# Eight tiles of first dots moved from ahead of the first spread into it, a quarter tile before each group

## The reference

```python
s = einsum('thpd,hpnd->thpn', (xb @ w_query), sub_keys)      # scores of 128 keys per half
top_s, top_i = top_k(s, 16)                                   # 16 best keys of each half
best_s, pos = top_k(top_s[0][:, None] + top_s[1][None, :], 16)
eid = key1 * 128 + key2                                       # expert number: two keys
gate = softmax(best_s)
z = einsum('thkd,td->thk', expert_down[eid], xb)              # the dots
out = einsum('thk,thkd->td', gate * gelu(z), expert_up[eid])  # the sums
```

## Time and profile before

| | |
|---|---|
| median of 3 runs | 4025.26 us (4020.61 to 4026.69) |
| the profiled execution, its own time | 4031.59 us |
| its span, from the first to the last instruction | 4029.8 us |
| PE busy | 3728.5 us, 93% of the span |
| DVE busy | 2323.1 us, 58% |
| ACT busy | 1266.1 us, 31% |
| share of PE in the chain that ended last | 86% |
| mean granted clock of TensorE | 0.932 of full speed |

### The profile page before, as it was taken

The page is one execution under the profiler, slowest core; times in us unless marked ns, Lnnn a source line. Parts: engine busy times, 40 slices in busy tenths (PEclk is TensorE's granted clock), DMA queues, the critical chain, the costliest instruction groups (busy, mean ns, idle before and its releaser), DMA issues.

```text
span 4029.8 us, 48913 instructions
## 1 busy us (share of the span) xinstructions
PE 3728.5 (93%) x14086; PEld 2386.4 (59%) x14086; DVE 2323.1 (58%) x4748; ACT 1266.1 (31%) x3367; POOL 658.0 (16%) x602
## 2 busy tenths in 40 slices
PE   7977999789999999997998899799589999999997
PEld 3443583576677777663444444347476677777764
DVE  1072696579877655664123400258978977755556
ACT  1141010357655454001011100101156755545201
POOL 0000001123433222220000000000113333311221
PEclk9988999669999999998997999899758999999998
DMA  3101148559999877993211112213657999977897
GB/s 131 64 20 52 63 169 362 198 204 388 379 392 400 342 298 299 396 383 133 73 63 47 42 73 73 84 61 120 258 188 289 386 377 394 391 300 301 343 384 284
DMA packets 129888, 926.81 MB, mean 230 GB/s; under 512 B 14800, under 2 KB 15744, under 8 KB 18184
## 3 DMA queue, kind: packets, MB, share of 16 engines
q0 software_dynamic: 73728, 536.90, 32.8%
q1 hardware_dynamic: 52368, 377.51, 24.4%
q10 hardware_dynamic: 3704, 11.36, 0.8%
HBM read 923.59 MB, written 2.12 MB: 230 GB/s over the span
## 4 chain that ended last, share of the span: by engine, by line
PE 86%; ACT 5%; DVE 5%; issue 2%; DMA 2%; ACTq 0%; DVEq 0%; POOL 0%; POOLq 0%; SPq 0%
PE proj L646 21%; PE proj L429 16%; PE obk L637 16%; PE tps L594 11%; PE proj L421 10%; PE proj L608 5%; ACT hot L920 2%; PE proj L578 2%; ACT hot L923 1%; DMA wring<-in_slabs 1%; PE tps L394 1%; PE obk L745 1%; DMA ring<-in_experts,idx 1%; DVE stat L1186 0%; PE proj L735 0%
## 5 line engine op out<-in xcount | busy, mean ns | idle before, releaser
L646 PE MATMUL proj<-wring,hT 128*128 128x512 f32 x2048 | 943.3, 604 | 1.8 <-DVE hT L1391 1.8
L374 POOL DMA_INDIRECT ring<-in_experts,idx x512 | 635.5, 1241 | 1766.1 <-DVE xn L1365 1655.9
L637 PE MATMUL obk<-hT,wring 128*128 128x256 f32 x3072 | 694.2, 379 | 0.0
L637 PEld LDWEIGHTS obk<-hT,wring 128*128 128x128 f32 x3072 | 583.5, 190 | 159.5 <-issue 89.5
L594 PEld LDWEIGHTS tps<-hT,hot 128*128 128x128 f32 x4096 | 601.0, 226 | 123.6 <-ACT hot L923 61.0
L594 PE MATMUL tps<-hT,hot 128*128 128x32 f32 x4096 | 597.8, 304 | 74.7 <-ACT hot L923 49.4
L1365 DVE SCALAR_TENSOR_TENSOR xn<-ring,coef,xn 128x1024 f32<-128x1024 f32 x512 | 628.7, 1280 | 22.4 <-DVE coef L1355 1.2
L1348 DVE SCALAR_TENSOR_TENSOR ring<-ring,xn 128x1024 f32<-128x1024 f32 x512 | 601.0, 1221 | 7.7 <-DMA ring<-in_experts,idx 7.6
L646 PEld LDWEIGHTS proj<-wring,hT 128*128 128x128 f32 x2048 | 377.0, 192 | 379.4 <-issue 372.6
L429 PE MATMUL proj<-hT,wring 128*128 128x512 f32 x1280 | 561.0, 596 | 9.2 <-DMA ring<-in_keys 5.2
L920 ACT ACTIVATE hot<-iota_sb,table 128x128 f32<-128x128 f32 x1792 | 567.1, 390 | 2.5 <-issue 1.3
(11 more groups left out here) (228 smaller groups left out, 2134.5 us busy)
## 6 DMA issues: line engine op xcount, KB each, us to landing
wring<-in_slabs SPq DMA_DIRECT2D x356, 1024.0 KB
ring<-in_experts,idx POOLq DMA_INDIRECT x512
x_res<-in_x SPq DMA_DIRECT2D x1, 2048.0 KB, 9.9
ring<-in_keys ACTq DMA_DIRECT2D x2, 1024.0 KB, 6.9
out<-x_res SPq DMA_DIRECT2D x4, 512.0 KB, 2.6
ring<-ada_rows ACTq DMA_DIRECT2D x1, 1536.0 KB, 6.3
ring<-in_norm_pre ACTq DMA_DIRECT2D x2, 512.0 KB, 7.2
ring<-ada_rows ACTq DMA_DIRECT2D x1, 1024.0 KB
```

Source lines behind the costliest of these rows:

```text
L374: pool.indirect_dma_start(rows[:, r, :], None, d[f"experts{layer + 1}"], bass.IndirectOffsetOnAxis(idx[:, k, r:r + 1], 0)).then_inc(row[r] ...
L637: m = pe.matmul(obk[:, j % 2, 0:DT], wring[:, k, at + c * P:at + (c + 1) * P], hT[:, c, GB * P:T], start=(c == 0), stop=(c == DC - 1))
L646: m = pe.matmul(proj[:, 2 * b + c, :], coef_t[:, j % 2, b * P:(b + 1) * P], wring[:, k, at + c * 512:at + (c + 1) * 512], start=False, sto ...
```

## The change

Pass 0's last 8 tiles (`ZB` = 2 tiles in each of 4 rounds) are taken out of `first_dots`, in both PEER layers. In the spread PE does two of the eight matmuls of such a tile before each group, so that a tile is done in four groups and a round has two tiles. ACT does the gelu of a tile after it has taken the group that follows its last quarter (`g % 4 == 3`). The 4 MB of `u` for these tiles form two slabs of their own (`S_ZB1`, `S_ZB2`), which stand behind the modulation's in the first layer; the first two slabs of the sums' experts are now loaded while the spread runs. The loop over rounds is written out in PE's stream. ACT no longer has 8 tiles' gelus between the gates and the first two `row_gelu`.

```diff
@@ -59,14 +59,18 @@
 assert FIRST_UNIT[CHUNKS] == UNITS and SGROUPS == BODY * STEPS
 
 
-N_IN1, N_OUT1, N_WQ, N_Z, N_ADA, N_CONV, N_QK, N_V, N_O, N_BR, N_OUT2 = 6, 2, 4, CK // 4, 12, 6, 2, 2, 2, 8, 2
-N_EXP = TILES // 2 - N_Z
+
+ZB = 2 * ROUNDS
+N_IN1, N_OUT1, N_WQ, N_ADA, N_CONV, N_QK, N_V, N_O, N_BR, N_OUT2 = 6, 2, 4, 12, 6, 2, 2, 2, 8, 2
+N_Z, N_ZB = (CK - ZB) // 4, ZB // 4
+N_EXP = TILES // 2 - N_Z - N_ZB
 S_IN1 = 0
 S_OUT1 = S_IN1 + N_IN1
 S_WQ1 = S_OUT1 + N_OUT1
 S_Z1 = S_WQ1 + N_WQ
 S_ADA = S_Z1 + N_Z
-S_EXP1 = S_ADA + N_ADA
+S_ZB1 = S_ADA + N_ADA
+S_EXP1 = S_ZB1 + N_ZB
 S_CONV = S_EXP1 + N_EXP
 S_QK2 = S_CONV + N_CONV
 S_V2 = S_QK2 + N_QK
...
@@ -343,11 +348,11 @@
             reload(S_IN1, N_IN1 + N_OUT1, True)
             reload(S_WQ1, N_WQ + N_Z, False)
             reload(S_ADA, N_ADA, True)
-            reload(S_EXP1, N_EXP + N_CONV + N_QK, False)
+            reload(S_ZB1, N_ZB + N_EXP + N_CONV + N_QK, False)
             reload(S_V2, N_V + N_O, True)
             reload(S_BR, N_BR, False)
             reload(S_OUT2, N_OUT2, True)
-            reload(S_WQ2, N_WQ + N_Z + N_EXP - PAIR, False)
+            reload(S_WQ2, N_WQ + N_Z + N_ZB + N_EXP - PAIR, False)
             with sp.Fori(0, TB) as tb:
                 sp.wait_ge(out_ready, tb + 1)
                 sp.dma_start(out[bass.ts(tb, P), :], x_res[:, bass.ds(tb, 1), :].rearrange("p b n -> p (b n)")).then_inc(stored, 16)
@@ -609,18 +614,32 @@
                                           start=(c == 0), stop=(c == DC - 1))
                         m.then_inc(mm_done, 1)
 
-            def experts(layer, first, job):
+            def experts(layer, first_zb, first, job):
 
                 pe.wait_ge(key_free, layer * HP + HP + 4)
                 pe.wait_ge(choice_set, layer + 1)
                 for b in range(TB - GB):
                     transposes(job + b, [choice[:, b, c, :] for c in range(3)])
                 pe.wait_ge(tr_free, job + 2)
-
-                with pe.Fori(0, ROUNDS) as it:
+                if layer == 0:
+                    all_read(S_EXP1)
+
+
+                for r in range(ROUNDS):
                     for g in range(RGROUPS):
-                        n = it * RGROUPS + g
-                        spread_group(n + layer * CHUNKS * SGROUPS, g % 2, (None, n + (layer * HOT2 + 1)))
+                        n = r * RGROUPS + g
+                        tile, at = divmod(g, RGROUPS // 2)
+                        if g == 0:
+                            half_landed(r, first_zb // PAIR)
+                        if at == 0:
+                            pe.wait_ge(z_act, layer * TILES + CK - ZB + 2 * r + tile - 1 + 4)
+                        for c in range(2 * at, 2 * at + 2):
+                            w = r % 2 * HALF + tile * D + c * P
+                            m = pe.matmul(proj[:, tile, 0:DT], wring[:, r // 2, w:w + P], hT[:, c, GB * P:T],
+                                          start=(c == 0), stop=(c == DC - 1))
+                        if c + 1 == DC:
+                            m.then_inc(mm_done, 1)
+                        spread_group(n + layer * CHUNKS * SGROUPS, g % 2, (None, n + layer * HOT2 + 1))
 
                 def spread_step(it, c, j):
 
@@ -648,8 +667,6 @@
                                           start=False, stop=False, skip_group_check=True)
                     m.then_inc(mm_done, jobs)
 
-                if layer == 0:
-                    all_read(S_EXP1)
                 pe.wait_ge(z_act, layer * TILES + CK + 4)
                 clear_sum(True)
 
@@ -690,10 +707,10 @@
             first_dots(0, S_Z1)
             pe.wait_ge(c_silu, 1)
             pe.wait_ge(in_bias, 16)
-            pe.wait_ge(z_act, CK + 4)
+            pe.wait_ge(z_act, CK - ZB + 4)
             for n in range(N_ADA):
                 modulation(n)
-            experts(0, S_EXP1, TR_T1)
+            experts(0, S_ZB1, S_EXP1, TR_T1)
 
 
             norm_transposes(TR_N2, xn, xn_ready, 2 * TB, 1)
...
@@ -929,8 +946,8 @@
 
             def modulation():
 
-                act.wait_ge(mm_done, 4 * S_EXP1)
-                act.activation(ada_rows, proj[0:N_ADA, 0, :].rearrange("p (k n) -> p k n", k=2), ACT.Copy).then_inc(mm_free, 4 * (N_Z + N_ADA))
+                act.wait_ge(mm_done, 4 * S_ZB1)
+                act.activation(ada_rows, proj[0:N_ADA, 0, :].rearrange("p (k n) -> p k n", k=2), ACT.Copy).then_inc(mm_free, 4 * (N_Z + N_ADA + N_ZB))
                 act.wait_ge(mm_free, 4 * S_EXP1 + 4)
                 act.dma_start(ada_dram.rearrange("o (p k n) -> (o p) k n", p=N_ADA, k=2), ada_rows).then_inc(ada_stored, 16)
                 act.wait_ge(ada_stored, 16)
...
@@ -951,11 +968,9 @@
                 gates(layer, 0)
                 first_gelus(8, 16)
                 gates(layer, 1)
-                first_gelus(16, 24)
+                first_gelus(16, CK - ZB)
                 gates(layer, GB)
-                first_gelus(24, 28)
                 row_gelu(layer, 0, 0, func)
-                first_gelus(28, 32)
                 row_gelu(layer, 0, 1, func)
                 gates(layer, GB + 1)
                 row_gelu(layer, 1, 0, func)
@@ -975,6 +990,11 @@
                         token = it * (RGROUPS * TG) + g * TG
                         hot2_half(layer, 0, n, 1, token, n + (layer * HOT2 + 1))
                         spread_take(layer, 0, n, g % 2, token)
+                        if g % 4 == 3:
+                            t = g // 4
+                            act.wait_ge(mm_done, it * 2 + (4 * first_zb + t + 1))
+                            act.activation(first_z[:, bass.ds(it * 2 + (CK - ZB + t), 1), :].rearrange("p i t -> p (i t)"), proj[:, t, 0:DT],
+                                           func).then_inc(z_act, 1)
                         if g % 4 == 1:
                             row_gelu(layer, it + ROUTED, g // 4, func)
                 for c in range(CHUNKS):
...
```

More of the change, by code:

```diff
@@ L77 @@
 S_Z2 = S_WQ2 + N_WQ
-S_EXP2 = S_Z2 + N_Z
+S_ZB2 = S_Z2 + N_Z
+S_EXP2 = S_ZB2 + N_ZB
 N_SLABS = S_EXP2 + N_EXP
@@ L940, in ada, with experts @@
                 return ada_dram[0:1, first * D:(first + n) * D].to_broadcast([P, n * D])
-            def experts(layer, first_z_slab, job, func):
+            def experts(layer, first_z_slab, first_zb, job, func):
                 def first_gelus(a, b):
@@ L1022, in _ @@
             act.dma_start(ada_bias, d["b_ada_2"]).then_inc(in_bias, 16)
-            experts(0, S_Z1, TR_T1, ACT.Gelu)
+            experts(0, S_Z1, S_ZB1, TR_T1, ACT.Gelu)
             rms(x_res, lambda tb: act.wait_ge(acc_free, tb + 1) if tb < GB else
@@ L1103, in _ @@
             route(1, S_WQ2)
-            experts(1, S_Z2, TR_T2, ACT.Gelu_apprx_tanh)
+            experts(1, S_Z2, S_ZB2, TR_T2, ACT.Gelu_apprx_tanh)
             act.wait_ge(slot_free, 2 * GB * SLOTS + RING)
@@ L1703, in lay_out @@
     slabs = np.concatenate([
-        by_rows(a["w_in"][0]), by_rows(a["w_out"][0]), by_tiles(columns(a["peer_w_query"][0])), first1, by_rows(a["w_ada_2"][0]),
-        rest1, by_tiles(conv), by_tiles(columns(q) + columns(k)), by_rows(v), by_rows(o), by_tiles(br), by_rows(a["w_out_2"][0]),
+        by_rows(a["w_in"][0]), by_rows(a["w_out"][0]), by_tiles(columns(a["peer_w_query"][0])), first1[:N_Z], by_rows(a["w_ada_2"][0]),
+        first1[N_Z:], rest1, by_tiles(conv), by_tiles(columns(q) + columns(k)), by_rows(v), by_rows(o), by_tiles(br), by_rows(a["w_out_2"][0]),
         by_tiles(columns(a["peer_wq_2"][0])), first2, rest2])
```

2 lines of the change are left out of this document (1 added, 1 removed).

## The result

| | before | changed |
|---|---|---|
| median | 4025.41 us (6 runs, 4020.61 to 4026.69) | 4040.32 us (6 runs, 4037.40 to 4047.48) |
| ratio | | 1.0045, 95% interval 1.0034 to 1.0055 |
| profiled execution, own time / span | 4031.59 / 4029.8 us | 4040.16 / 4038.4 us |
| mean granted clock | 0.932 | 0.925 |

The change costs 14.9 us by the medians; 17.3 were predicted. The spans differ by only 8.6 us, because the profiled execution of before lay 6.2 us above its median and that of the changed kernel at its own. Some kernels of the experiments have executions of two kinds, some 95 us apart; for these every execution is told, and the ratio and its interval count the shorter kind alone.

A forecast was written before the change was run, and what follows sets the result against it. PE bounds the first layer's dots, DVE the second layer ahead of its spread, a PE-ACT loop the spread. First layer -2.8 and second +20.1 give +17.3 us on 4025.3: 4043 us, range 4022 to 4058 for 8 times in 10.

The forecast's parts named there:

- DVE's wait: Second layer, ahead of the spread: DVE's wait for ACT's gelu of half a row unit goes away, -3.6 us.
- The period: Spread of both layers: one group takes 5.17 us instead of 4.38, costing +24.5 and +23.4 us.
- PE goes from second to first: In the spread PE becomes the bound and no longer waits; its 0.71 us to spare per period are used up.
- The first layer's gain: Ahead of the first layer's spread: 8 of 32 tiles of dots removed, -27.6 us.
- the modulation's waits for slabs: First layer's modulation: PE's 8.3 us of waits for slabs stay as they are, 0, with bounds of -8.3 and +8.3.
- the 15 that were to be a sign of being wrong: Modulation: waits for slabs above 15 us were listed among the signs that the forecast is wrong.
- one more burst comes inside it: Modulation: one more burst of three gathers falls into it, besides those of row units 1 and 2; costed at 0.
- more is paid: Rival: modulation waits twice as long for slabs (+8.3) and the spread's period is 5.35 us (+11); 4062 us, chance 0.08.
- The second layer: DVE is the bound ahead of its spread, so little comes back: -3.6 + 23.4 + 0.3 = +20.1 us.
- The clock: Both spreads: the granted clock stays at 0.50 although PE has no gap left; the whole sum supposes this.
- a risen clock: Rival: dots bring both spreads to 1.00, period 3.7 us, total -73 us, 3952 us; chance 0.09.
- the rivals: Clock rises (3952 us, 0.09), clock goes up and down (3999, 0.09), more paid (4062, 0.08), dots hidden (shows as risen clock).

The follow-up runs named there:

- e5: The changed kernel with one moved matmul instead of two ahead of each group, 4 of the 8 tiles done ahead of the spread; 4006.12 us, ratio 0.9953.
- e9: The change in the first layer only, with an ACT wait there that splits the six gathers into three and three; 4021.09 us.
- e1: The change in the first layer only, the second layer as in the kernel before; 4022.82 us, ratio 0.9999.
- e2: The change in the second layer only, against the kernel before; 4042.86 us, ratio 1.0042.
- e10: Kernel before, no dots moved; ACT's wait for the modulation rows' store made later, half a row unit's gelu made earlier; 4013.84 us, ratio 0.9968.
- e8: The changed kernel plus 10 and 6 unread dense matmuls of 256 columns up to group 0, both layers; 4039.63 us, ratio 1.0038 against before.
- e4: Sixteen tiles moved instead of 8, four matmuls ahead of each group, both layers; 3928.64, 4026.89, 3927.07, 4019.82 us; shorter two 0.9757 against before.
- e12: Repeat of e7's kernel for more executions; three of seven at 4017.54 to 4021.55 us, the shorter four at ratio 0.9747 against before.
- e7: Sixteen tiles moved, four matmuls per group, unread dense matmuls up to group 0, ACT's store wait made later; 3924.74 to 3930.15 us, ratio 0.9755.
- e3: Kernel before plus four unread matmuls of 256 columns ahead of each group of the first spread, both layers; 4076.57 us, ratio 1.0124.

## Why the prediction was right

The mechanism and the side were right, and each step can be set beside what it met. That the total came so near is in part luck. In the traces the touched stages sum to +19.6 us where +17.3 were predicted: 6.5 us of modulation that the sum had at 0, less 3.7 us by which the spreads and 0.6 by which DVE's wait came out better. The medians, at +14.9, miss the prediction by 2.4 us to the other side.

- **The period.** Predicted 5.17 us from 2 x 1.71 + 1.73 = 5.15 at the low end; measured 5.12 (3.25 + 1.87). The spread's part was 0.17 smaller than twice 1.71 and the dots' 0.14 larger than 1.73. Over 31 and 30 periods the 0.05 are 3 us in sum, of the 3.7 by which the two spreads came out cheaper. That PE goes from second to first showed as 0.71 us of waiting gone, and e5 shows the limit from the other side: with one matmul the period stays at 4.34. The spread was 164.9 us long in the first layer and 165.2 in the second, where about 165 were said.
- **The first layer's gain.** 27.6 us of dots out: exact. The step that was mis-sized is the modulation's waits for slabs, taken as 0 with bounds of 8.3 both ways. They rose by 6.2 us to 14.5, inside the bound and just under the 15 that were to be a sign of being wrong, and the whole stage by 6.5. With it the first layer's spread started at 718.3 and its pass 0 at 883.1, not near 711 and 877 as said. The reason given, "the same slabs and nearly the same gathers share the same stretch", was wrong in its second half: the slabs were the same 24 MB, the gathered rows 15.4 MB and not 11.3. ACT's new order also draws the gathers together (e9: about 1.7 us of e1's 4.6). The prediction's own remark that one more burst comes inside it was the hint. One half of the rival *more is paid* thus came three quarters of its way (6.2 of 8.3 us), while its other half, the period of 5.35, did not.
- **The second layer.** e2 shows that the loss is all there, as the sum had it (+20.1 against -2.8). DVE's wait was -4.2 in the trace, -3.8 in e10, for 3.6 predicted.
- **The clock.** The forecast hung on 0.50, and both spreads were at 0.50 in full. The rule of the Trainium skill ("TensorE: Matmul & The Clock Gate", section "Why this matters for your kernels"), keep TensorE busy without a break and it gets to the full clock, did not hold here: PE was busy for 163.93 of 164.80 us at 0.50. The prediction's own reason, that what PE does counts and not only that it is busy, fits e8, which entered at 1.00 and fell back, and e4, where four dense matmuls per group ran at 1.00. It is not the whole of it: in e12 the same four matmuls per group kept PE busy for 195.00 of 195.00 us at 0.50.
- **What it had wrong about the rival.** Its time for a risen clock, 3952 us, was for a state that two matmuls per group didn't hold. That the same work could stand at either level for a whole spread, 96 us apart, was in none of the rivals.

## What to carry to other kernels

Work moved under another engine's shadow is free only up to what the engine stands still per period, at the clock that it has there: take the period, subtract what the engine's own work takes when it runs without a break, divide by the cost of a piece at that clock, and move no more (here (4.38 - 3.25) / 0.93, one matmul and not two). Moving more can pay only if the clock rises with it, and here that was not sure (e4). Where PE's waiting for DVE is the path, nothing moved off PE is won, while an instruction order on the engine in between can be (DVE's wait in e10). A stretch with the DMA engines at 0.92 of their time can get longer when the one ahead of it gets shorter, since other transfers then fall into it: here 4.1 MB of gathered rows more, and 4.6 to 6.5 us. Count the bytes that will land in it, not only those that it asks for.

## What the hardware showed that was not expected

One and the same loop has two lasting states. With four matmuls of 256 columns ahead of each group's eight of 32, the second spread ran at 1.00 (120.1 us in e7) or at 0.50 (216.1 us in e12), in different executions of one kernel. With two matmuls per group the spreads of the changed kernel, of e1 and of e2 were at 0.50 throughout, and e8's fell back to it after an entry at 1.00. Behind a wait of 2.99 us on PE the clock was at 0.50 in e12 and in e7, and only in e7's profiled execution it came back; what makes the difference is open. So work added to a stretch can shorten it: with e3's four matmuls that nobody reads the first layer, from its first dots to its first sums, was 23.0 us shorter than before at 1.00, and the second 74.7 us longer at 0.50, in one and the same execution. Moving dots to the same places made the kernel 2.4% faster or left it where it was (e4: 3928 or 4020 to 4027 us), and a single execution doesn't tell which of the two a kernel does.
